# A one-layer streaming encoder step: gain as a column on transposed rows, first weight blocks in halves, key loads split into groups

## Chip, cores, metric

One core of a Trainium2 chip runs the whole kernel. The metric is device time in microseconds, the median of repeated executions; the profile is of one further execution.

## The reference

One layer of a hybrid encoder on 512 prompt rows and 64 sample rows of width 1024 (float32):

```python
h = rmsnorm(x, g_mix)                        # x * rsqrt(mean(x^2)) * g_mix
rq, rk, rv, rg, dq, dk, dv, gr, gd = split(h @ w_in)       # w_in: 1024 x 8192
dq, dk = rmsnorm per head (g_q, g_k)         # 4 heads, 2 maps of 128
o_r = chunkwise retention(rq, rk, rv)
o_d = differential attention(dq, dk, dv)     # sample rows also see 512 cached keys
x = x + (sig(gr) * out_r + sig(gd) * out_d) @ w_out
x = x + hier_moe(rmsnorm(x, g_ffn))          # 16 experts, two for each row
```

Outputs are y, the new keys and values, and the retention states.

## The kernel before

Rows are in five tiles of 128 (`TT` = 5; tile 4, `PT`, holds the 64 sample rows). Products are made in a split float32 form: each operand is stored as a high part (rounded to fp32r) and a low part (the rest), and `product` (L467) issues three matmuls, high by high, low by high, high by low. For tile 4 high and low rows lie side by side in one stationary operand, so two matmuls do (L1792, L1793).

The 8192 columns of `w_in` are taken as 16 chunks of 512 columns. A chunk has two 1 MB blocks, numbered n = 2c and 2c + 1, each with 4 of the 8 contraction steps. SyncE loads blocks into four slots of `raw`; ScalarE rounds a block to `w_hi` (`dense_hi`, L393), VectorE subtracts to `w_lo` (`dense_lo`, L402, written in place), TensorE uses it for five tiles (`dense`, L1771: 24 matmuls for a tile, 16 for tile 4).

Before the first chunk the input is prepared. VectorE multiplies each tile of `x_tok` by the gain `gmix`, spread over all partitions, into one of two `h_tok` buffers (`gained`, L1271). TensorE transposes it in two halves of four 128 x 128 transposes (`source`, L1757; `ident` is the first part of the constant tile `gen`), ScalarE copies each half from PSUM to `s_hi` (`source_hi`), VectorE makes `s_lo` (`source_lo`). The order on each engine is written out by hand: TensorE does tiles 0 and 1, then `dense` of tile 0, the transposes of tiles 2 and 3, `dense` of tile 1, the transposes of tile 4. The row norm (`x_rstd`, from squares that ScalarE sums, `square_x`) is applied later, as a scale when ScalarE evacuates a product (`evacuate_z`, L913), so no product leaves PSUM before it is there. After it VectorE clears three staging regions and casts two constants (L1298 to L1300), and then works on chunk 0: for each of the first tiles a square and a reduce, and the low parts of blocks 2 and 3 behind tiles 1 and 2. Products alternate between PSUM banks 0 and 1.

Chunks 8 to 11 are interleaved with attention: unit g = 5h + t does for head h and tile t the transposed mix of the unit before, `scores`, a share of the transposes of the next head's queries and keys (`head_part`; parts 0 to 6, at t = 1: 0 and 1, t = 2: 2 and 3, t = 3: 4 and 5, t = 4: 6), then `dense` for one tile and the weighted values of the unit before. Parts 0 and 3 read the prompt keys `k_tok`, 1 and 4 the cached keys `kc_tok`, 2 and 5 the prompt queries `q_tok`, 6 the sample rows of both. These tiles exist once, so the loads for head h + 2 (`load_keys`, L632: four DMAs, issued by GpSimd) wait until part 6 of head h + 1 is evacuated, in the unit with t = 4, ahead of that unit's store of its product. TensorE waits before part 0 for all four:

```python
        def head_part(h, k):
            if k == 0:
                pe.wait_ge(kq_in, 64 * (h + 1))
```

After attention come retention, the output products, routing and the 16 experts. At the very end GpSimd waits for the last scattered rows (`all_landed(0)`, L861).

Of the kernel before, what the change touches and what calls it, by code (L numbers as in the profile page):

```python
# [14 lines left out]
P = 128  # L15
D_MODEL = 1024
PROMPT = 512
# [96 lines left out]
def build(nc, a, o):  # L114
# [55 lines left out]
    h_tok = after("h_tok", [P, 2, D_MODEL], f32)  # L170
    gmix = after("gmix", [P, D_MODEL], f32)
# [129 lines left out]
    gmix_in, gen_in, x_scaled = sem("gmix_in"), sem("gen_in"), sem("x_scaled")  # L301
# [9 lines left out]
    kq_in, lam_loaded = sem("kq_in"), sem("lam_loaded")  # L311
# [205 lines left out]

    def source_unit(s, t):
        return 2 * TT * s + 2 * (ORDER.index(t) if s == 4 else t)
# [9 lines left out]
    def _(sp):  # L529
        def dense_load(n):  # L530
            if n == LAST:
                sp.wait_ge(state_stored, 32 * H)
            elif n > LAST:
                sp.wait_ge(src_ready, 3 * TT)
# [79 lines left out]
        with sp.If(passes > 1):  # L614
            with sp.Fori(1, passes) as j:
                expert_pass(j)


    @block.gpsimd
    def _(pool):  # L620
# [10 lines left out]

        def load_keys(h):  # L632
            lo, up = h * DV, (h + 1) * DV
            dma(k_tok[:, 0:PT, :], tiles(z["k"], lo, up, 0, PT)).then_inc(kq_in, 16)
            dma(k_tok[0:SAMPLE, PT, :], z["k"][PROMPT:REAL, lo:up]).then_inc(kq_in, 16)
            dma(kc_tok[:, :, :], a["cache_k"][0, 0, :, h, :].rearrange("(t p) c -> p t c", p=P)).then_inc(kq_in, 16)
            dma(q_tok[:, :, :], tiles(z["q"], lo, up)).then_inc(kq_in, 16)
# [57 lines left out]
        for u in range(TT * PURE, TT * IN_CHUNKS):  # L695
# [3 lines left out]
            if g < UNITS:  # L699
                if t == PT and h + 2 < H:  # L700
                    pool.wait_ge(tr_evacuated, small_n["head", h + 1, HEAD_USES - 1] + 1)
                    load_keys(h + 2)
                if t == 1:
                    if h == 0:
                        for s in range(3):
                            pool.wait_ge(stage_stored[s], stored(PURE - 1, s))
                    else:
                        pool.wait_ge(av_ready, TT * h)
                        load_cached_values(h)
                    if h + 1 < H:  # L710
# [12 lines left out]
                if g == 16:  # L723
                    pool.wait_ge(av_ready, 15)
                    for k in range(TT):
                        pool.wait_ge(ring_stored[k], 32)
                    load_ret_values(0)
            else:
                r = g - UNITS
                h = r // TT  # L730
                if r == 1:
                    pool.wait_ge(av_ready, UNITS)
                    load_state(0)
                    load_ret_values(1)
                if r in (2, 7):
                    pool.wait_ge(kw_ready, h + 1)
                    pool.wait_ge(tr_evacuated, small_n["ret", h, 2] + 1)
                    load_ret_keys(h + 2)
                if t == 0 and h >= 1:
                    pool.wait_ge(state_evacuated, TT * h)  # L740
                    load_state(h)
                    if h + 1 < H:
                        load_ret_values(h + 1)
                    store_states(h - 1)
                if r == 17:
                    pool.wait_ge(kw_ready, H)
# [21 lines left out]
        pool.wait_ge(src_ready, 2 * TT)  # L768
# [4 lines left out]
        pool.wait_ge(src_ready, 3 * TT)  # L773
# [87 lines left out]
        all_landed(0)  # L861
# [3 lines left out]
    def _(act):  # L865
# [9 lines left out]
        def lower_half(bank):  # L875
            nc.scalar.copy(fold[:, :], ps[SAMPLE:P, bank, :]).then_inc(fold_ready, 1)  # L876

# [30 lines left out]
        root()  # L908
        source_hi(0, 4)
# [3 lines left out]
        def evacuate_z(c, t):  # L913
# [15 lines left out]
            if t < PT:  # L929
                nc.scalar.activation(dst[:, t, :], ps[:, u % 2, :], func,  # L930
                                     scale=x_rstd[:, t:t + 1]).then_inc(z_evacuated, 1)
            else:
                if c:
                    act.wait_ge(z_evacuated, TT * c)
                lower_half(u % 2)
# [299 lines left out]
    def _(dve):  # L1235
# [27 lines left out]
        def sum_dense(c):  # L1263
            sum_halves((TT * c + PT) % 2, c).then_inc(folded, 1)
# [6 lines left out]
        def gained(t):  # L1271
            dve.wait_ge(x_in[t], 16)
            if t == PT:
                dve.wait_ge(x_padded, 1)
            if t >= 2:
                dve.wait_ge(src_transposed, 2 * (t - 1))
            v.tensor_tensor(h_tok[:, t % 2, :], x_tok[:, t, :], gmix[:, :], ALU.mult).then_inc(src_ready, 1)
# [17 lines left out]
        source_lo(0, 4)  # L1295
# [221 lines left out]
        def router_weights():  # L1517
            dve.wait_ge(router_in, 80)
            dve.wait_ge(src_ready, 2 * TT)
# [234 lines left out]
    def _(pe):  # L1754
        mm, transpose = nc.tensor.matmul, nc.tensor.transpose

        def source(s, t, src):  # L1757

            for half in range(2):
# [3 lines left out]
                deep = 3 if s == 0 else 2  # L1763
                if u >= deep:
                    pe.wait_ge(slo_ready, u - deep + 1)
# [5 lines left out]
        def dense(s, c, t, ready, within=None):  # L1771
# [4 lines left out]
            pe.wait_ge(slo_ready, 2 * TT * s + 2 * (t + 1))  # L1776
            if u >= 2:
                if u < TT * IN_CHUNKS + 2:
# [3 lines left out]
            bank, rows = ps[:, u % 2, :], slice(t * P, (t + 1) * P)  # L1782
            for k in range(KC):
# [3 lines left out]
                if t == 0 and kk == 0:  # L1787
                    pe.wait_ge(lo_ready, n + 1)
# [7 lines left out]
                if k == 3 and within is not None:  # L1796
                    route(within)
# [19 lines left out]
        def head_part(h, k):  # L1817
            if k == 0:
                pe.wait_ge(kq_in, 64 * (h + 1))
# [65 lines left out]
        pe.wait_ge(gen_in, 16)  # L1885

        def first_source(t):
            pe.wait_ge(src_ready, t + 1)
            source(0, t, h_tok[:, t % 2, :])

        first_source(0)
        first_source(1)
        for c in range(PURE):
            for t in range(TT):
# [3 lines left out]
                dense(0, c, t, z_ready)  # L1898
                if c == 0:
                    for k in ((2, 3), (4,), (), (), ())[t]:  # L1900
                        first_source(k)
# [58 lines left out]
        def attended_source(t):  # L1960
            pe.wait_ge(src_ready, TT + t + 1)
# [19 lines left out]
        def next_source(x, t):  # L1981

            if x == 1:
                pe.wait_ge(src_ready, 2 * TT + t + 1)
# [40 lines left out]
        for n, t in enumerate(ORDER):  # L2025
            dense(3, IN_CHUNKS + 4, t, p_ready, within=n)
# [143 lines left out]
_INS = ["x_prompt", "x_sample", "cache_k", "cache_v", "state_ret", "g_mix", "w_in", "g_q", "g_k", "lambda_q1",  # L2170
# [24 lines left out]
```

## Time and profile before

| what | value |
|---|---|
| median of 3 runs | 1052.09 us (1050.88 to 1052.38) |
| profiled execution | 1057.25 us, of which its span is 1055.4 us |
| TensorE busy | 1012.0 us, 96% of the span |
| VectorE busy | 677.4 us, 64% |
| ScalarE busy | 529.0 us, 50% |
| GpSimd busy | 146.7 us, 14% |
| mean granted TensorE clock | 0.985 of full |

TensorE is busy nearly all the time, so the places to look at are the few where it is not. Times below count from the start of the span. A difference between two kernels' spans is set against the difference of their medians, since the profiled execution is some 5 us longer than the median.

### The profile page before, as it was taken

The numbers are of one execution on the slowest core, as the hardware profiler recorded it, in microseconds if no ns is written. First come the engines' busy times: TensorE is split into PE (matmuls) and PEld (weight loads), VectorE is DVE, ScalarE is ACT, GpSimd is POOL, SyncE is SP. The second block draws the span as 40 slices with busy tenths as digits, with TensorE's granted clock in tenths as the row PEclk, the third lists the DMA queues.
The fourth block names the chain that finished last, engine by engine and source line by source line (L and its number), as shares of the span: only waits on it lengthen the run. The fifth ranks groups of instructions, "written<-read, shape, count | busy, mean of one in ns | idle before, by whom it ended". The sixth has DMA issues, their size and how long they took to land.

```text
span 1055.4 us, 12423 instructions
## 1 busy us (share of the span) xinstructions
PE 1012.0 (96%) x4780; PEld 832.6 (79%) x4780; DVE 677.4 (64%) x990; ACT 529.0 (50%) x726; POOL 146.7 (14%) x181
## 2 busy tenths in 40 slices
PE   4999999999999999999999999998999999999996
PEld 3788888888777888788778888887778888888784
DVE  5677775226555664345246655687699898888882
ACT  4433322446454554333353223364587877868772
POOL 1000011111202121211112000011211211212112
PEclk9999999999999999999999999998899999999998
DMA  9238856262615334424347434227799999999994
GB/s 304 67 143 305 306 216 221 94 247 86 215 41 210 112 143 140 141 110 160 125 160 262 157 125 160 101 102 270 303 425 381 405 384 404 396 392 405 383 368 63
DMA packets 62180, 238.20 MB, mean 226 GB/s; under 512 B 5392, under 2 KB 5568, under 8 KB 49792
## 3 DMA queue, kind: packets, MB, share of 16 engines
q1 hardware_dynamic: 41152, 163.32, 40.5%
q0 software_dynamic: 20960, 73.99, 21.1%
q8 instruction: 40, 0.66, 0.2%
q14 instruction: 28, 0.23, 0.1%
HBM read 199.92 MB, written 48.15 MB: 235 GB/s over the span
## 4 chain that ended last, share of the span: by engine, by line
PE 62%; issue 25%; DMA 5%; POOL 3%; DVE 3%; ACT 1%; SPq 0%; POOLq 0%; ACTq 0%; DVEq 0%
PE ps L469 15%; PE ps L471 15%; PE ps L470 15%; PE ps L1792 3%; PE ps L1793 3%; PE ps L1811 2%; DMA q_tok<-z_q 2%; PE ps L1768 2%; PE ps L1848 1%; POOL x_exp L800 1%; POOL out_y L811 1%; DMA rows_a<-x_slots 1%; DMA x_tok<-in_x_prompt 1%; PE ps L1941 1%; PE ps L1957 1%
## 5 line engine op out<-in xcount | busy, mean ns | idle before, releaser
L469 PE MATMUL ps<-w_hi,s_hi 128*128 128x512 f32 x672 | 268.1, 399 | 1.4 <-ACT stage L930 1.1
L471 PE MATMUL ps<-w_lo,s_hi 128*128 128x512 f32 x672 | 263.4, 392 | 0.0
L470 PE MATMUL ps<-w_hi,s_lo 128*128 128x512 f32 x672 | 263.2, 392 | 0.0
L469 PEld LDWEIGHTS ps<-w_hi,s_hi 128*128 128x128 f32 x672 | 127.4, 190 | 27.5 <-DVE s_hi L1255 1.4
L471 PEld LDWEIGHTS ps<-w_lo,s_hi 128*128 128x128 f32 x672 | 126.9, 189 | 26.9
L470 PEld LDWEIGHTS ps<-w_hi,s_lo 128*128 128x128 f32 x672 | 127.2, 189 | 25.5 <-issue 0.2
L930 ACT ACTIVATE stage<-ps,x_rstd 128x512 f32<-128x512 f32 x64 | 43.9, 688 | 188.3 <-PE ps L471 188.3
L405 DVE TENSOR_TENSOR w_lo<-raw,w_hi 128x2048 fp32r<-128x2048 f32 x42 | 96.2, 2290 | 44.6 <-ACT w_hi L400 44.4
L400 ACT CAST w_hi<-raw 128x2048 fp32r<-128x2048 f32 x42 | 80.0, 1909 | 15.3 <-DMA raw<-in_w_in 10.0
L441 DVE TENSOR_TENSOR lo_x<-raw_x,w_hi 128x2048 fp32r<-128x2048 f32 x32 | 72.1, 2287 | 10.8 <-ACT w_hi L418 10.8
L441 DVE TENSOR_TENSOR lo_x<-raw_x,hi_x 128x2048 fp32r<-128x2048 f32 x32 | 72.2, 2287 | 8.6 <-ACT hi_x L418 8.5
L471 PE MATMUL ps<-lo_x,x_hi 128*128 128x512 f32 x192 | 75.7, 394 | 0.0
L418 ACT CAST w_hi<-raw_x 128x2048 fp32r<-128x2048 f32 x32 | 60.4, 1916 | 16.3 <-DMA raw_x<-in_w_down 12.9
L811 POOL DMA_INDIRECT out_y<-y_exp,s_idx x15 | 35.5, 2363 | 237.7 <-ACT y_exp L1186 237.7
L418 ACT CAST hi_x<-raw_x 128x2048 fp32r<-128x2048 f32 x32 | 60.3, 1916 | 13.2 <-DMA raw_x<-in_w_down 12.4
L1792 PE MATMUL ps<-w_hi,s_hi 128*128 128x512 f32 x168 | 66.6, 396 | 0.0
L1793 PE MATMUL ps<-w_lo,s_hi 128*128 128x512 f32 x168 | 65.5, 390 | 0.0
L469 PE MATMUL ps<-w_hi,x_hi 128*128 128x512 f32 x136 | 54.8, 403 | 1.4 <-issue 1.2
L470 PE MATMUL ps<-w_hi,x_lo 128*128 128x512 f32 x136 | 54.2, 399 | 0.0
L884 ACT CAST s_hi<-ps 128x512 fp32r<-128x512 f32 (+1 forms) x50 | 25.3, 546 | 54.8 <-PE ps L1768 54.5
L469 PE MATMUL ps<-hi_x,x_hi 128*128 128x512 f32 x128 | 51.0, 398 | 1.2 <-DVE x_lo L1690 0.7
L1261 DVE TENSOR_TENSOR fold<-ps,fold 64x512 f32<-64x512 f32 x22 | 15.0, 681 | 52.0 <-ACT fold L876 52.0
(306 smaller groups left out, 1859.2 us busy)
## 6 DMA issues: line engine op xcount, KB each, us to landing
raw<-in_w_in SPq DMA_DIRECT2D x32, 1024.0 KB, 7.3
raw_x<-in_w_up SPq DMA_DIRECT2D x30, 1024.0 KB, 20.4
raw_x<-in_w_down SPq DMA_DIRECT2D x18, 1024.0 KB, 20.8
raw<-in_w_gate SPq DMA_DIRECT2D x16, 1024.0 KB, 19.2
raw_x<-in_w_gate SPq DMA_DIRECT2D x16, 1024.0 KB, 19.8
raw<-in_w_down SPq DMA_DIRECT2D x14, 1024.0 KB, 21.6
x_slots<-in_c_empty SPq DMA_DIRECT2D x4, 2112.0 KB, 16.4
x_exp<-x_slots POOLq DMA_DIRECT2D x16, 528.0 KB, 13.0
```

What stands on the lines that cost most here:

```text
L400: nc.scalar.copy(hi_slots[dense_hi_at(n)], raw_slots[dense_raw(n)]).then_inc(hi_ready, 1)
L405: nc.vector.tensor_tensor(lo_slots[dense_raw(n)], raw_slots[dense_raw(n)], hi_slots[dense_hi_at(n)].bitcast(f32), ALU.subtract).then_inc(l ...
L418: nc.scalar.copy(hi_of(i, q), raw_of(i, q)).then_inc(hi_ready, 1)
L441: nc.vector.tensor_tensor(lo_of(i, q), raw_of(i, q), hi_of(i, q).bitcast(f32), ALU.subtract).then_inc(lo_ready, 1)
L469: nc.tensor.matmul(out, s_h, w_h, start=first, stop=False)
L470: nc.tensor.matmul(out, s_l, w_h, start=False, stop=False)
L471: return nc.tensor.matmul(out, s_h, w_l, start=False, stop=last)
L811: pool.indirect_dma_start(out=y_dram, out_offset=bass.IndirectOffsetOnAxis(ap=s_idx[:, i:i + 1], axis=0), in_=y_exp[i % 2][:, :], in_offse ...
L884: nc.scalar.copy(s_hi[:, 4 * half:4 * half + 4, t * P:t * P + rows], ps[:, source_bank(u), :].rearrange("p (k c) -> p k c", k=4)[:, :, 0:r ...
L930: nc.scalar.activation(dst[:, t, :], ps[:, u % 2, :], func, scale=x_rstd[:, t:t + 1]).then_inc(z_evacuated, 1)
L1792: mm(bank, s_hi[:, k, rows], w_h, start=k == 0, stop=False)
L1793: last = mm(bank, s_hi[:, k, rows], w_l, start=False, stop=k == KC - 1)
```

## The change

In the prologue the gain is no longer applied to rows. TensorE transposes `x_tok` itself, and VectorE multiplies each transposed half in PSUM by the gain as a column (`gmix_col`, 128 partitions x 8) into one of four buffers `h_half`; `s_hi` and `s_lo` are made from there. The identity is loaded alone, ahead of the rest of `gen`. Blocks 0 and 1 are loaded, rounded and subtracted in halves with semaphores of their own. Tile 1 is transposed in the middle of the first tile's product, tiles 2, 3 and 4 behind tiles 0, 1 and 2. Eight transposes of the identity follow those of tile 0. Chunk 0 has a PSUM bank for each tile. Key loads are split: prompt keys in the unit with t = 3, cached keys and prompt queries in that with t = 4 behind part 5, sample rows behind part 6 with a semaphore of their own. At the end SyncE waits for the scattered rows in place of GpSimd. `src_ready` counts five less everywhere, since it is no longer raised in the prologue.

```diff
+    def z_bank(u):
+        return u if u < TT else u % 2
...
+        def first_load(n):
+            for half, landed in enumerate((raw_early[n], raw_full[n])):
+                sp.dma_start(raw[:, n, half * (BLK // 2):(half + 1) * (BLK // 2)].rearrange("p (k c) -> p k c", k=2),
+                             chunk_block(n)[:, 2 * half:2 * half + 2, :]).then_inc(landed, 16)
         load_x(0)
-        sp.dma_start(gmix[:, :], a["g_mix"][0].partition_broadcast(P)).then_inc(gmix_in, 16)
-        dense_load(0)
-        sp.dma_start(gen[:, :], a["c_gen"]).then_inc(gen_in, 16)
+        sp.dma_start(ident, a["c_gen"][:, 0:P]).then_inc(ident_in, 16)
+        sp.dma_start(gmix_col[:, :], a["g_mix_col"]).then_inc(gmix_in, 16)
+        first_load(0)
         load_x(1)
-        dense_load(1)
+        first_load(1)
         load_x(2)
         load_x(3)
         sp.dma_start(x_tok[0:SAMPLE, PT, :], a["x_sample"][0]).then_inc(x_in[PT], 16)
+        sp.dma_start(gen[:, P:], a["c_gen"][:, P:]).then_inc(gen_in, 16)
...
+        sp.wait_ge(y_half_landed, 16)
+        for k in range(2):
+            sp.wait_ge(y_scattered[k], 16 * (NE // 2))
...
+                if t == 3 and h + 2 < H:
+                    pool.wait_ge(tr_evacuated, small_n["head", h + 1, 3] + 1)
+                    load_prompt_keys(h + 2)
                 if t == PT and h + 2 < H:
+                    pool.wait_ge(tr_evacuated, small_n["head", h + 1, 5] + 1)
+                    load_cached_keys(h + 2)
+                    load_prompt_queries(h + 2)
                     pool.wait_ge(tr_evacuated, small_n["head", h + 1, HEAD_USES - 1] + 1)
-                    load_keys(h + 2)
+                    load_sample_keys(h + 2)
...
-        all_landed(0)
...
-        dense_hi(act, 0)
-        source_hi(0, 0)
-        dense_hi(act, 1)
+        first_hi(0, 0)
+        gained_hi(0)
+        gained_hi(1)
+        first_hi(0, 1)
+        gained_hi(2)
+        first_hi(1, 0)
+        gained_hi(3)
+        first_hi(1, 1)
         act.wait_ge(x_padded, 1)
         square_x(0)
-        source_hi(0, 1)
+        gained_hi(4)
+        gained_hi(5)
         square_x(1)
         square_x(2)
+        gained_hi(6)
+        gained_hi(7)
         square_x(3)
-        source_hi(0, 2)
         square_x(4)
-        source_hi(0, 3)
+        gained_hi(8)
+        gained_hi(9)
         root()
-        source_hi(0, 4)
...
+        def gained(u):
+            half = u % 2
+            dve.wait_ge(src_transposed, u + 1)
+            if u >= 4:
+                dve.wait_ge(slo_ready, u - 3)
+            v.tensor_tensor(h_half[:, u % 4, :, :], ps[:, source_bank(u), :].rearrange("p (k c) -> p k c", k=4),
+                            gmix_col[:, 4 * half:4 * half + 4].unsqueeze(2).to_broadcast([P, KC // 2, P]),
+                            ALU.mult).then_inc(x_gained, 1)
...
         dve.wait_ge(gmix_in, 16)
         gained(0)
         gained(1)
-        dense_lo(dve, 0)
-        source_lo(0, 0)
-        dense_lo(dve, 1)
-        source_lo(0, 1)
+        first_lo(0, 0)
+        gained_lo(0)
+        gained_lo(1)
+        first_lo(0, 1)
         gained(2)
         gained(3)
-        source_lo(0, 2)
-        gained(4)
-        source_lo(0, 3)
+        first_lo(1, 0)
+        gained_lo(2)
+        gained_lo(3)
+        first_lo(1, 1)
+        for u in (4, 6, 8):
+            gained(u)
+            gained(u + 1)
+            gained_lo(u)
+            gained_lo(u + 1)
         dve.wait_ge(x_squared, TT)
...
-        source_lo(0, 4)
...
+        pe.wait_ge(ident_in, 16)
         first_source(0)
-        first_source(1)
+        for k in range(8):
+            transpose(ps[:, 4, (k % 4) * P:(k % 4 + 1) * P], ident, ident)
...
+                if c == 0 and t < 3:
+                    dense(0, c, t, z_ready, within=(lambda: first_source(1)) if t == 0 else None)
+                    first_source(t + 2)
```

## Rows read from the trace of the kernel before

**Rows 1.** Waits of TensorE over the run: in total, times, longest

```profile
PE ps L1811 <- DMA q_tok<-z_q: 4.5, 2, 2.5
```

**Rows 2.** POOL, then ScalarE, about unit 3; landing of the q_tok loads

```profile
262.49 0.54 POOL L753 DMA_DIRECT2D z_rv<-stage  x1 [8.31 <-ACT stage L930]
...
271.89 0.89 POOL L637 DMA_DIRECT2D q_tok<-z_q  x1
...
259.31 0.60 ACT L945 COPY qT<-ps 128x512 f32<-128x512 f32 x1
...
DMA to landing us min/median/max: 8.1/10.0/10.9
```

**Rows 3.** TensorE in units 1, 6 and 11: scores, then the next mix; a window's clock

```profile
236.56 1.03 PE L1848 MATMUL ps<-kT,qT 128*128 128x256 f32 x4
...
244.26 0.38 PE L1811 MATMUL ps<-gen,prob 128*128 128x128 f32 x2
...
279.32 1.03 PE L1848 MATMUL ps<-kT,qT 128*128 128x256 f32 x4
...
291.11 0.38 PE L1811 MATMUL ps<-gen,prob 128*128 128x128 f32 x2
...
326.10 1.03 PE L1848 MATMUL ps<-kT,qT 128*128 128x256 f32 x4
...
337.49 0.38 PE L1811 MATMUL ps<-gen,prob 128*128 128x128 f32 x2
...
279.00:284.00 5.00, 2.50 (x13) 0.86 0.91 326
```

**Rows 4.** Issues of the prologue, KB, us to landing; last, landing of gffn_col

```profile
x_tok<-in_x_prompt SPq DMA_DIRECT2D x1, 512.0 KB, 3.6
...
gmix<-in_g_mix SPq DMA_DIRECT2D x1, 512.0 KB, 5.3
...
raw<-in_w_in SPq DMA_DIRECT2D x1, 1024.0 KB, 9.1
...
raw<-in_w_in SPq DMA_DIRECT2D x1, 1024.0 KB, 12.0
...
gffn_col<-in_g_ffn_col POOLq DMA_DIRECT2D x1, 4.0 KB, 10.5
```

**Rows 5.** Timeline of the prologue up to the last transposes

```profile
10.77 1.90 ACT L400 CAST w_hi<-raw 128x2048 fp32r<-128x2048 f32 x1 [8.75 <-DMA raw<-in_w_in]
11.31 1.97 PE L1768 MATMUL ps<-gen,h_tok 128*128 128x128 f32 x8 [11.31 <-DMA gen<-in_c_gen]
...
15.92 1.28 DVE L1255 TENSOR_TENSOR s_lo<-ps,s_hi 128x512 fp32r<-128x512 f32 x2
...
17.43 0.78 PE L469 MATMUL ps<-w_hi,s_hi 128*128 128x512 f32 x1
...
18.43 0.63 PE L471 MATMUL ps<-w_lo,s_hi 128*128 128x512 f32 x1
...
32.09 1.04 PE L1768 MATMUL ps<-gen,h_tok 128*128 128x128 f32 x8
```

**Rows 6.** Timeline from the root's table load to the end of chunk 0

```profile
27.85 1.28 ACT L873 ACT_TABLE_LOAD   x1
...
34.15 0.48 DVE L1298 MEMSET stage<- 64x512 f32 x1 [0.16 <-issue]
34.27 0.47 PE L469 MATMUL ps<-w_hi,s_hi 128*128 128x512 f32 x1 [1.14 <-ACT stage L930]
...
39.39 2.29 DVE L405 TENSOR_TENSOR w_lo<-raw,w_hi 128x2048 fp32r<-128x2048 f32 x1
...
43.04 2.29 DVE L405 TENSOR_TENSOR w_lo<-raw,w_hi 128x2048 fp32r<-128x2048 f32 x1
...
48.63 0.39 PE L1793 MATMUL ps<-w_lo,s_hi 128*128 128x512 f32 x1
```

**Rows 7.** The last compute instruction of the timeline

```profile
1046.26 1.54 POOL L818 DMA_INDIRECT out_y<-y_exp,s_half  x1 [1.44 <-ACT y_exp L1186]
```

More of the change, by code:

```diff
@@ L169, in build @@
     x_tok = at("x_tok", [P, TT, D_MODEL], f32, X + 30720)
-    h_tok = after("h_tok", [P, 2, D_MODEL], f32)
-    gmix = after("gmix", [P, D_MODEL], f32)
+    h_half = after("h_half", [P, 4, KC // 2, P], f32)
+    gmix_col = after("gmix_col", [P, KC], f32)
     sq_x = at("sq_x", [P, D_MODEL], f32, X + 98304)
@@ L300, in build @@
     hi_ready, lo_ready, blocks_used = sem("hi_ready"), sem("lo_ready"), sem("blocks_used")
-    gmix_in, gen_in, x_scaled = sem("gmix_in"), sem("gen_in"), sem("x_scaled")
+    gmix_in, ident_in, gen_in, x_scaled = sem("gmix_in"), sem("ident_in"), sem("gen_in"), sem("x_scaled")
+    raw_early, hi_early, lo_early = [sem("raw_early0"), sem("raw_early1")], sem("hi_early"), sem("lo_early")
+    x_gained = sem("x_gained")
     rot_in, ret_in, router_in = sem("rot_in"), sem("ret_in"), sem("router_in")
@@ L310, in build @@
     ring_stored = [sem(f"ring_stored{t}") for t in range(TT)]
-    kq_in, lam_loaded = sem("kq_in"), sem("lam_loaded")
+    kq_in, kq_rest_in, lam_loaded = sem("kq_in"), sem("kq_rest_in"), sem("lam_loaded")
     v_in, vc_in = [sem("v_in0"), sem("v_in1")], sem("vc_in")
@@ L533, in dense_load @@
             elif n > LAST:
-                sp.wait_ge(src_ready, 3 * TT)
+                sp.wait_ge(src_ready, 2 * TT)
             elif n >= WR:
@@ L630, in _, with load_prompt_keys, load_cached_keys, load_prompt_queries @@
         dma(r_bias[:, NG:NG + NE], a["b_expert"][0].partition_broadcast(P)).then_inc(rot_in, 16)
-        def load_keys(h):
[L633 to L637, printed above, removed]
+        def load_prompt_keys(h):
+            dma(k_tok[:, 0:PT, :], tiles(z["k"], h * DV, (h + 1) * DV, 0, PT)).then_inc(kq_in, 16)
+        def load_cached_keys(h):
+            dma(kc_tok[:, :, :], a["cache_k"][0, 0, :, h, :].rearrange("(t p) c -> p t c", p=P)).then_inc(kq_in, 16)
+        def load_prompt_queries(h):
+            dma(q_tok[:, 0:PT, :], tiles(z["q"], h * DV, (h + 1) * DV, 0, PT)).then_inc(kq_in, 16)
+        def load_sample_keys(h):
+            lo, up = h * DV, (h + 1) * DV
+            dma(k_tok[0:SAMPLE, PT, :], z["k"][PROMPT:REAL, lo:up]).then_inc(kq_rest_in, 16)
+            dma(q_tok[:, PT, :], z["q"][PROMPT:ROWS, lo:up]).then_inc(kq_rest_in, 16)
+        def load_keys(h):
+            load_prompt_keys(h)
+            load_cached_keys(h)
+            load_prompt_queries(h)
+            load_sample_keys(h)
         def load_values(h):
@@ L767, in _ @@
         dma(gffn[:, :], a["g_ffn"][0].partition_broadcast(P)).then_inc(router_in, 16)
-        pool.wait_ge(src_ready, 2 * TT)
+        pool.wait_ge(src_ready, TT)
         dma(count_up[:, :], a["c_count"]).then_inc(router_in, 16)
@@ L772, in _ @@
         dma(w_r[:, :, NG:NG + NE], a["w_expert"][0].rearrange("(k p) c -> p k c", p=P)).then_inc(router_in, 16)
-        pool.wait_ge(src_ready, 3 * TT)
+        pool.wait_ge(src_ready, 2 * TT)
         load_gate("gr", 1, 2)
@@ L876, in lower_half, with first_hi, gained_hi @@
             nc.scalar.copy(fold[:, :], ps[SAMPLE:P, bank, :]).then_inc(fold_ready, 1)
+        def first_hi(n, half):
+            cols = slice(half * (BLK // 2), (half + 1) * (BLK // 2))
+            act.wait_ge(raw_full[n] if half else raw_early[n], 16)
+            nc.scalar.copy(w_hi[:, n, cols], raw[:, n, cols]).then_inc(hi_ready if half else hi_early, 1)
+        def gained_hi(u):
+            t, half = divmod(u, 2)
+            rows = P if t < PT else SAMPLE
+            act.wait_ge(x_gained, u + 1)
+            nc.scalar.copy(s_hi[:, 4 * half:4 * half + 4, t * P:t * P + rows], h_half[:, u % 4, :, 0:rows])\
+                .then_inc(shi_ready, 1)
         def source_hi(s, t):
@@ L929, in evacuate_z @@
             if t < PT:
-                nc.scalar.activation(dst[:, t, :], ps[:, u % 2, :], func,
+                nc.scalar.activation(dst[:, t, :], ps[:, z_bank(u), :], func,
                                      scale=x_rstd[:, t:t + 1]).then_inc(z_evacuated, 1)
@@ L934, in evacuate_z @@
                     act.wait_ge(z_evacuated, TT * c)
-                lower_half(u % 2)
+                lower_half(z_bank(u))
                 act.wait_ge(folded, c + 1)
@@ L1263, in sum_dense @@
         def sum_dense(c):
-            sum_halves((TT * c + PT) % 2, c).then_inc(folded, 1)
+            sum_halves(z_bank(TT * c + PT), c).then_inc(folded, 1)
         own(v.memset(stat[:, :, :, :], 1.0))
@@ L1268, in _, with gained_lo, first_lo @@
         v.memset(x_tok[SAMPLE:P, PT, :], 0.0).then_inc(x_padded, 1)
[L1271 to L1277, printed above, removed]
+        def gained(u):
[6 more added lines that the diff above has]
+                            ALU.mult).then_inc(x_gained, 1)
+        def gained_lo(u):
+            t, half = divmod(u, 2)
+            ks, rows = slice(4 * half, 4 * half + 4), P if t < PT else SAMPLE
+            hi = s_hi[:, ks, t * P:t * P + rows]
+            lo = s_lo[:, ks, t * P:t * P + rows] if t < PT else s_hi[:, ks, t * P + rows:t * P + 2 * rows]
+            dve.wait_ge(x_gained, u + 1)
+            dve.wait_ge(shi_ready, u + 1)
+            v.tensor_tensor(lo, h_half[:, u % 4, :, 0:rows], hi.bitcast(f32), ALU.subtract).then_inc(slo_ready, 1)
+        def first_lo(n, half):
+            cols = slice(half * (BLK // 2), (half + 1) * (BLK // 2))
+            dve.wait_ge(hi_ready if half else hi_early, n + 1)
+            v.tensor_tensor(w_lo[:, n, cols], raw[:, n, cols], w_hi[:, n, cols].bitcast(f32), ALU.subtract)\
+                .then_inc(lo_ready if half else lo_early, 1)
         dve.wait_ge(gmix_in, 16)
@@ L1518, in router_weights @@
             dve.wait_ge(router_in, 80)
-            dve.wait_ge(src_ready, 2 * TT)
+            dve.wait_ge(src_ready, TT)
             own(v.tensor_tensor(w_r[:, :, :], w_r[:, :, :], gffn_col[:, :].unsqueeze(2).to_broadcast([P, KC, NR]),
@@ L1762, in source @@
                     pe.wait_ge(tr_evacuated, len(small))
-                deep = 3 if s == 0 else 2
-                if u >= deep:
-                    pe.wait_ge(slo_ready, u - deep + 1)
+                if s == 0 and u >= 3:
+                    pe.wait_ge(x_gained, u - 2)
+                elif s:
+                    pe.wait_ge(slo_ready, u - 1)
                 for k in range(4):
@@ L1775, in dense @@
             ends = t == (ORDER[-1] if x >= 4 else PT)
-            pe.wait_ge(slo_ready, 2 * TT * s + 2 * (t + 1))
-            if u >= 2:
-                if u < TT * IN_CHUNKS + 2:
+            if u:
+                pe.wait_ge(slo_ready, 2 * TT * s + 2 * (t + 1))
+            if u >= TT:
+                if u < TT + 2:
+                    pe.wait_ge(z_evacuated, u - 3)
+                elif u < TT * IN_CHUNKS + 2:
                     pe.wait_ge(z_evacuated, u - 1)
@@ L1781, in dense @@
                     pe.wait_ge(p_evacuated, u - TT * IN_CHUNKS - 1)
-            bank, rows = ps[:, u % 2, :], slice(t * P, (t + 1) * P)
+            bank, rows = ps[:, z_bank(u), :], slice(t * P, (t + 1) * P)
             for k in range(KC):
@@ L1786, in dense @@
                 w_h, w_l = hi_slots[dense_hi_at(n)][:, cols], lo_slots[dense_raw(n)][:, cols]
-                if t == 0 and kk == 0:
+                if u == 0 and kk == 0:
+                    pe.wait_ge(slo_ready, half + 1)
+                    pe.wait_ge(lo_early, n + 1)
+                if t == 0 and kk == (2 if u == 0 else 0):
                     pe.wait_ge(lo_ready, n + 1)
@@ L1796, in dense @@
                 if k == 3 and within is not None:
-                    route(within)
+                    within()
             if not ends:
@@ L1818, in head_part @@
             if k == 0:
-                pe.wait_ge(kq_in, 64 * (h + 1))
+                pe.wait_ge(kq_in, 48 * (h + 1))
+            if k == HEAD_USES - 1:
+                pe.wait_ge(kq_rest_in, 32 * (h + 1))
             if k < 6:
@@ L1882, in weighted_values @@
             last.then_inc(av_ready, 1)
-        pe.wait_ge(gen_in, 16)
         def first_source(t):
-            pe.wait_ge(src_ready, t + 1)
-            source(0, t, h_tok[:, t % 2, :])
+            pe.wait_ge(x_in[t], 16)
+            if t == PT:
+                pe.wait_ge(x_padded, 1)
+            source(0, t, x_tok[:, t, :])
+        pe.wait_ge(ident_in, 16)
         first_source(0)
-        first_source(1)
+        for k in range(8):
+            transpose(ps[:, 4, (k % 4) * P:(k % 4 + 1) * P], ident, ident)
         for c in range(PURE):
@@ L1897, in _ @@
                         head_part(0, k)
[L1898 to L1901, printed above, removed]
+                if c == 0 and t < 3:
+                    dense(0, c, t, z_ready, within=(lambda: first_source(1)) if t == 0 else None)
+                    first_source(t + 2)
+                else:
+                    dense(0, c, t, z_ready)
         for g in range(UNITS):
@@ L1960, in attended_source @@
         def attended_source(t):
-            pe.wait_ge(src_ready, TT + t + 1)
+            pe.wait_ge(src_ready, t + 1)
             source(1, t, od[:, t, :])
@@ L1983, in next_source @@
             if x == 1:
-                pe.wait_ge(src_ready, 2 * TT + t + 1)
+                pe.wait_ge(src_ready, TT + t + 1)
                 source(2, t, ro[:, t, :])
@@ L2025, in _ @@
         for n, t in enumerate(ORDER):
-            dense(3, IN_CHUNKS + 4, t, p_ready, within=n)
+            dense(3, IN_CHUNKS + 4, t, p_ready, within=lambda: route(n))
             if n == 0:
@@ L2167, in stored @@
     return sum(32 if SECTION[k][0] in ("k", "v") else 16 for k in range(min(c + 1, PURE)) if k % 3 == s)
-_INS = ["x_prompt", "x_sample", "cache_k", "cache_v", "state_ret", "g_mix", "w_in", "g_q", "g_k", "lambda_q1",
+_INS = ["x_prompt", "x_sample", "cache_k", "cache_v", "state_ret", "w_in", "g_q", "g_k", "lambda_q1",
         "lambda_k1", "lambda_q2", "lambda_k2", "g_ret", "w_ret_o", "g_sub", "w_diff_o", "w_out", "g_ffn", "w_group",
@@ L2182 @@
     arrays, ins = {}, {}
-    by_row = {"g_ffn_col": inputs["g_ffn"].reshape(KC, P).T}
+    by_row = {"g_mix_col": inputs["g_mix"].reshape(KC, P).T, "g_ffn_col": inputs["g_ffn"].reshape(KC, P).T}
     for name, arr in [(n, inputs[n]) for n in _INS] + list(by_row.items()) + list(shape_constants().items()):
```

## Prediction

> **What bounds the kernel now.** I read the shares of the page first: TensorE works 96% of the span, so no other engine's saving counts unless it closes a gap of TensorE's. Then its waits, then the timeline at each. Three kinds matter here. It does nothing for the first 11.3 us and reaches the first product at 17.43 [rows 5]. It waits 4.5 us in two places for the load of the queries [rows 1]. And its matmuls are slow for a while behind a gap. Everything else is back to back, so a gap closed at 280 us should be kept to the end.
>
> **The key loads.** Units 1, 6 and 11 do the same work (tile 1 of heads 0, 1, 2, each with parts 0 and 1 of the next head). From scores to the next mix unit 1 takes 244.26 - 236.56 = 7.70 us, unit 6 takes 291.11 - 279.32 = 11.79 and unit 11 takes 337.49 - 326.10 = 11.39 [rows 3]. Units 6 and 11 contain the two waits [rows 1]. The excess is 4.09 + 3.69 = 7.8 us: 4.5 of waiting, and 3.3 of matmuls and transposes at the lower clock behind it (granted clock 0.86 in the mean over 279 to 284, that is, partly at 1.2 in place of 2.4 GHz [rows 3]). What does the change do to it? The query load was issued at 271.89, last of four, behind part 6 of unit 4. It is now the second of two behind part 5, whose evacuation ended at 259.9; GpSimd gets there when its store of unit 3 is issued, 262.49 + 0.54, so the queries go out at 263.03 + 0.8 = 263.8, 8.1 us sooner; prompt keys a whole unit before that [rows 2]. With the slowest landing, 10.9 us, they are there at 274.7; TensorE wants them at 280.4. A margin of 5.7 us: both waits go, and with them the slow stretches. I take the whole 7.8. The lower bound is the waits without the clock, 4.5. The new waits of GpSimd are for evacuations that are over when it comes to them, so the stores queued behind (z_rv) go out no later; behind part 6 two DMAs are issued where there were four, so that store goes about 2 us sooner. Heads 0 and 1 cost one DMA more each, 0.5 us of GpSimd, long before use. The wait for the sample rows stands at part 6, three units behind part 0. What is late next in units 6 and 11? The same unit in head 0 shows no wait, and the weight blocks were loading together with the keys (DMA share 0.91 in the row [rows 3]), which now pass earlier; I find nothing.
>
> **The prologue, start.** Landings: x of tile 0 at 0.74 + 3.6 = 4.3, gain at 1.20 + 5.3 = 6.5, block 0 at 10.8, block 1 at 15.2 [rows 4, 5]. In the queue the gain (512 KB) and the constants (218 KB) stood ahead of what is needed; now 64 KB and 4 KB do. So the first half of block 0 ends about where the gain ended, 512 KB behind x: 6.5, I take 6.9 for the two small loads; its second half 2.1 later (half of the 4.3 from gain to block 0), 9.0. For the column nothing like it is in the trace but gffn_col, of the same 128 rows of 32 bytes, 10.5 us on GpSimd's queue [rows 4]. Bounds: issued at 1.65, it lands between 5.3 (with the 3.6 of x) and 12.2; I take 6, since little stands ahead of it.
>
> The ladder: transposes from about 4.8, 8 at low clock take 1.97 [rows 5], halves ready at 5.9 and 6.8. The multiply from PSUM over 128x512 should cost what the subtraction from PSUM does, 0.65 [rows 5]: 6.65 and 7.5. ScalarE rounds a half block (half of 1.90, about 1.0) to 7.9, VectorE subtracts it (half of 2.29, 1.15) to 9.05, the low half tile to 9.7. **TensorE starts its product at 9.75, 7.7 us sooner than at 17.43.** Its first six matmuls at 0.43 apart (17.99 to 18.43 and on, slow [rows 5]) last to 12.3, six more at full rate to 13.7; VectorE has the second half block ready by 11.6. Full rate is 0.228: 64 matmuls of tiles 2 to 4 from 34.27 to 48.86 [rows 6].
>
> **The prologue, the return.** Now tile 1 is transposed (halves ready 14.3, 14.75), VectorE multiplies both (15.6), ScalarE rounds the first (15.55), and only then the first half of block 1 (16.6): low part 17.75. TensorE has stood since about 14.8, 3 us. Six matmuls, slow again, to 20.4; the second half of block 1 is ready at 20.2 (VectorE has two low half tiles in between, 0.65 each); the last six end at 22.4. Call this E. Neither x of tile 1 nor block 1 is late in it: block 1 landed at 15.2 even before [rows 4].
>
> Behind E: transposes (1.0 for 8 [rows 5]), tile 1 (24 x 0.228 = 5.46), transposes, tile 2, then tile 4's transposes at E + 12.9, now one tile later than before. Call it T. VectorE multiplies its halves (T + 2.0), ScalarE rounds them (T + 2.45), loads the root's table (1.28 [rows 6]), and the root gives x_rstd at T + 4.2. VectorE clears from T + 4.35. From there the low part of block 2 ended 39.39 + 2.29 - 34.15 = 7.5 later and that of block 3 11.2 later [rows 6]: T + 11.9 and T + 15.5. TensorE has only 1.0 + 5.46 + 3.64 = 10.1 us of chunk 0 left behind T. **So chunk 1 waits: 1.8 us for block 2, 1.0 for block 3.** Before, chunk 1 began at 48.86 with both ready since 45.3 [rows 6]. Now it goes as if begun at T + 15.5 - 2.73 = E + 25.7 = 48.1. Net gain of the whole prologue: 0.8 us, of the 7.7 at the start. The separate banks keep TensorE from the wait of 1.14 at 34.27 [rows 6] (counted, since I run chunk 0 without it). Bounds: if the first matmuls run at full clock, E is 20.4 and the gain 2.8; if the column lands at 12.2, product 0 begins at 14.1, E is near 27 and the prologue loses 3.8.
>
> On the eight transposes of the identity: before, TensorE ran transposes from 11.31 on, with gaps, and the matmuls at 17.43 and 18.43 were still slow [rows 5]. So I count no help from them. The page "TensorE: Matmul & The Clock Gate" of the Trainium skill, in its section "PE-mode transpose", says that transposes do not count as busy for the clock gate the way matmuls do. By that rule the eight are of no use and the forecast stands; if they count, it is the case of 2.8. The trace agrees with the page so far.
>
> **The end.** The last instruction begins at 1046.26, the span ends 9.1 us later [rows 7]; its landing must be waited for by someone. Which engine waits I price at nought; bounds 0 to 1 us of gain, since only the engines' closing steps could overlap with it.
>
> **Sum.** 7.8 + 0.8 = 8.6 us. Profiled execution: 1057.25 - 8.6 = 1048.6, span 1046.8. That execution stands 5.2 us over the median; I take the difference over: 1052.1 - 8.6 = **1043.5**.
>
> **Rivals.**
> (a) The start is kept: the clock is up at the first product. For it: sixteen transposes without a gap, where there were eight. Against: the slow matmuls at 17.43 behind transposes [rows 5]. 7.8 + 2.8: 1041.5. Chance 0.17.
> (b) The column is late, as gffn_col. 7.8 - 3.8 = 4.0: 1048.1. Against it: loads in the prologue land when the bytes ahead of them have passed, and only 0.6 MB are ahead of the column; the 10.5 us of gffn_col for 4 KB must be mostly other loads' time. Chance 0.09.
> (c) The queries' wait goes but another, of a block's split or a value load, takes half of it: 3.9 + 0.8: 1047.4. Chance 0.07.
> (d) The other side: the ladder of TensorE, VectorE, ScalarE, VectorE on each half tile repeats for tiles 2 to 4 and pushes the root, and with it blocks 2 and 3, back. It decides when E or T comes 8.6 us later than I have them (E at 31). That needs each of some eight handovers at double its price, against rows of 0.65 and 1.0 us: 1053 or more. Chance 0.03 slower, 0.03 for no change.
> The forecast, 0.61, its own range 1042.3 to 1045.
>
> A measurement of this kernel tells about 0.2%, 2.1 us, from no change. All but (d) is faster by more: 0.94, 0.03, 0.03. The range: from (a) with the gain at the end, 1040.7, to most of the way to (c), 1046.5.
>
> **What would show it.** Right: no wait of L1811 for q_tok; units 6 and 11 near 7.7 us; first product near 9.8; a gap of 3 us in the middle of tile 0; a gap at the start of chunk 1 with VectorE's low part as its releaser. Wrong: gmix_col as a releaser; a wait near 280; chunk 1 starting without a gap.

## Result and the profile after

| | before | changed |
|---|---|---|
| median, 12 runs each | 1052.03 us (1049.84 to 1057.29) | 1047.94 us (1046.07 to 1050.50) |
| ratio, 95% interval | 1 | 0.995 (0.9935 to 0.9965) |
| profiled execution | 1057.25 us, span 1055.4 | 1049.38 us, span 1047.5 |

The change is worth 4.1 us by the medians and 0.5%, 5.3 us (3.7 to 6.8), by the ratio; 8.6 were forecast. The two profiled executions differ by 7.9. That is nearly the forecast, and it misleads: the profiled execution of before took 1057.25 us, and of the kernel's 12 others only one took longer (1057.29). It stood 5.2 us over its median; that of the changed kernel stands 1.4 us over.

TensorE's waits of the changed kernel (in total, times, longest), where [rows 1] stood before:

```profile
PE ps L1843 <- DMA gen<-in_c_gen: 4.7, 1, 4.7
PE ps L471 <- DVE w_lo L1345: 3.3, 1, 3.3
...
PE ps L471 <- DVE w_lo L407: 1.8, 1, 1.8
...
PE ps L471 <- DVE s_lo L1340: 1.6, 1, 1.6
```

No wait for q_tok is left. Three new ones, all in the prologue, name VectorE. TensorE's timeline shows them in place, first the products of tile 0 (start, duration, in brackets the idle time before and what ended it), then the transposes of tiles 2 and 4 and the first product of chunk 1:

```profile
4.72 1.97 PE L1843 MATMUL ps<-gen,x_tok 128*128 128x128 f32 x8 [4.72 <-DMA gen<-in_c_gen]
...
10.03 0.80 PE L471 MATMUL ps<-w_hi,s_hi 128*128 128x512 f32 x1 [1.64 <-DVE s_lo L1340]
...
14.89 0.63 PE L473 MATMUL ps<-w_lo,s_hi 128*128 128x512 f32 x1
15.32 1.37 PE L1843 MATMUL ps<-gen,x_tok 128*128 128x128 f32 x8
...
19.99 0.76 PE L471 MATMUL ps<-w_hi,s_hi 128*128 128x512 f32 x1 [3.29 <-DVE w_lo L1345]
...
24.13 1.04 PE L1843 MATMUL ps<-gen,x_tok 128*128 128x128 f32 x8
...
36.81 1.04 PE L1843 MATMUL ps<-gen,x_tok 128*128 128x128 f32 x8
...
48.77 0.47 PE L471 MATMUL ps<-w_hi,s_hi 128*128 128x512 f32 x1 [1.84 <-DVE w_lo L407]
```

The product starts at 10.0 where [rows 5] had 17.43, and it is given back step by step: still at 0.63 a matmul (the low clock) at 14.89, 3.29 us of waiting in the middle of tile 0, 1.84 at chunk 1. VectorE behind it, the clears and the low parts of blocks 2 and 3, beside [rows 6]:

```profile
41.09 0.48 DVE L1372 MEMSET stage<- 64x512 f32 x1 [0.16 <-issue]
...
46.33 2.29 DVE L407 TENSOR_TENSOR w_lo<-raw,w_hi 128x2048 fp32r<-128x2048 f32 x1
...
49.98 2.29 DVE L407 TENSOR_TENSOR w_lo<-raw,w_hi 128x2048 fp32r<-128x2048 f32 x1
```

Units 6 and 11 beside [rows 3], and the issue of the queries beside [rows 2]:

```profile
280.98 1.03 PE L1931 MATMUL ps<-kT,qT 128*128 128x256 f32 x4
...
288.57 0.38 PE L1892 MATMUL ps<-gen,prob 128*128 128x128 f32 x2
...
323.59 1.03 PE L1931 MATMUL ps<-kT,qT 128*128 128x256 f32 x4
...
331.16 0.38 PE L1892 MATMUL ps<-gen,prob 128*128 128x128 f32 x2
```
```profile
264.66 0.76 POOL L651 DMA_DIRECT2D kc_tok<-in_cache_k  x1
265.41 0.76 POOL L654 DMA_DIRECT2D q_tok<-z_q  x1
```

Both units take 7.6 us. The queries go out 15.6 us ahead of unit 6's scores, where before it was 7.4.

### The profile page after: what moved, and what is told of

It is laid out like the page before. It is cut to its first block, busy times and chain, and to the rows that moved or that the text cites. A ratio compares the mean times of both kernels' runs of the same rounds, so it can differ in the third digit from the quotient of the medians.

```text
span 1047.5 us, 12470 instructions
## 1 busy us (share of the span) xinstructions
PE 1014.2 (97%) x4788; PEld 835.0 (80%) x4788; DVE 678.3 (65%) x997; ACT 529.4 (51%) x728; POOL 147.6 (14%) x185
## 4 chain that ended last, share of the span: by engine, by line
PE 63%; issue 25%; DVE 3%; POOL 3%; ACT 1%; POOLq 0%; ACTq 0%; DVEq 0%
PE ps L471 15%; PE ps L473 15%; PE ps L472 15%; PE ps L1873 3%; PE ps L1874 3%; PE ps L1892 2%; PE ps L1931 2%; PE ps L1843 2%; POOL x_exp L834 1%; POOL out_y L845 1%; PE ps L2027 1%; PE ps L2043 1%; PE ps L2034 1%; PE ps L1935 1%; PE ps L2013 1%
## 5 line engine op out<-in xcount | busy, mean ns | idle before, releaser
L472 PEld LDWEIGHTS ps<-w_hi,s_lo 128*128 128x128 f32 x672 | 127.7, 190 | 25.7 <-issue 0.2
L407 DVE TENSOR_TENSOR w_lo<-raw,w_hi 128x2048 fp32r<-128x2048 f32 x40 | 91.6, 2290 | 42.0 <-ACT w_hi L402 41.7
L402 ACT CAST w_hi<-raw 128x2048 fp32r<-128x2048 f32 x40 | 76.2, 1909 | 5.9 <-DMA raw<-in_w_out 3.3
L443 DVE TENSOR_TENSOR lo_x<-raw_x,w_hi 128x2048 fp32r<-128x2048 f32 x32 | 72.1, 2287 | 10.6 <-ACT w_hi L420 10.6
L845 POOL DMA_INDIRECT out_y<-y_exp,s_idx x15 | 35.0, 2333 | 237.6 <-ACT y_exp L1238 237.6
L472 PE MATMUL ps<-hi_x,x_lo 128*128 128x512 f32 x120 | 47.2, 394 | 0.0
## 6 DMA issues: line engine op xcount, KB each, us to landing
raw_x<-in_w_gate SPq DMA_DIRECT2D x16, 1024.0 KB, 19.4
```

Source lines behind the costliest of these rows:

```text
L402: nc.scalar.copy(hi_slots[dense_hi_at(n)], raw_slots[dense_raw(n)]).then_inc(hi_ready, 1)
L407: nc.vector.tensor_tensor(lo_slots[dense_raw(n)], raw_slots[dense_raw(n)], hi_slots[dense_hi_at(n)].bitcast(f32), ALU.subtract).then_inc(l ...
L443: nc.vector.tensor_tensor(lo_of(i, q), raw_of(i, q), hi_of(i, q).bitcast(f32), ALU.subtract).then_inc(lo_ready, 1)
L472: nc.tensor.matmul(out, s_l, w_h, start=False, stop=False)
L845: pool.indirect_dma_start(out=y_dram, out_offset=bass.IndirectOffsetOnAxis(ap=s_idx[:, i:i + 1], axis=0), in_=y_exp[i % 2][:, :], in_offse ...
```

## Experiments

All ratios are to the kernel before, run on the same chip, with 95% intervals; "traces" are one profiled execution for each kernel. `before_copy`, the same program as before, came out at 1.0012 (1.0000 to 1.0024), so a difference of 0.1% in a ratio says nothing.

**The parts alone.** `keys_only` is the kernel before with the key loads of the change; `prologue_only` is the changed kernel with the key loads and the final wait of before; `end_only` is the kernel before with the final wait on SyncE; `before_copy` is unchanged.

```diff
 keys_only (to before)
+                if t == 3 and h + 2 < H:
+                    pool.wait_ge(tr_evacuated, small_n["head", h + 1, 3] + 1)
+                    load_prompt_keys(h + 2)
...
 prologue_only (to the changed kernel)
-                    load_sample_keys(h + 2)
+                    load_keys(h + 2)
...
 end_only (to before)
-        all_landed(0)
+        sp.wait_ge(y_half_landed, 16)
```

> The kernel before with only the key loads split into groups. Theory A (the whole difference between the profiled spans, 7.9 us, is the key loads; the prologue gives nothing): 7 to 8 us faster than before in the median, waits on q_tok gone, units 6 and 11 at 7.7 us from scores to the next mix. Theory B (the profiled execution of before was a long one; in most executions the waits for the queries are shorter, or no slow stretch stands behind them): the waits gone, but only 4 to 6 us faster in the median.

> The changed kernel with the key loads and the final wait as before, so that only the prologue is changed. Theory A: nothing in the median (within 1 us of before). Theory B (the prologue loses what its trace shows, 1.6 us at the start of unit 1, by two further slow stretches of the clock): 1.5 to 2 us slower than before. My prediction had 0.8 us faster.

> The kernel before with only the final wait moved from GpSimd to SyncE. By my prediction nothing (0 to 1 us faster). The profiled spans of before and after differ by 2 us behind the last expert's gate; if that is this wait, the median falls by 1 to 2 us; if it is chance of one execution, by nothing.

> The kernel before, unchanged, to see how much one execution differs from another. If the two waits for the queries with their slow stretches are typical, units 6 and 11 take 11.4 to 11.8 us again and the span is near 1050 to 1055 us. Theory B expects them shorter, 9 to 10.5 us, in this trace. Ratio to before 1.000 within 0.2%.

| kernel | median us | ratio (interval) |
|---|---|---|
| keys_only | 1048.73 | 0.9951 (0.9938 to 0.9964) |
| prologue_only | 1054.40 | 1.0007 (0.9995 to 1.0019) |
| end_only | 1053.20 | 0.9998 (0.9986 to 1.0010) |
| before_copy | 1054.51 | 1.0012 (1.0000 to 1.0024) |

The key loads alone are worth 0.49%, 5.2 us (3.8 to 6.5). The prologue alone, for which the table has +0.7 us (0.5 faster to 2.0 slower), gives no gain that can be seen and may cost. The final wait can't be told from nothing. The product of the three ratios is 0.9956, the changed kernel's own is 0.995. Theory B holds for the keys. It shows in the trace of before_copy, first its waits, then units 6 and 11, then TensorE's clock (the third column behind the window) in the stretches behind the waits:

```profile
PE ps L1811 <- DMA q_tok<-z_q: 3.1, 2, 1.8
```
```profile
279.98 1.03 PE L1848 MATMUL ps<-kT,qT 128*128 128x256 f32 x4
...
289.00 0.38 PE L1811 MATMUL ps<-gen,prob 128*128 128x128 f32 x2
...
324.03 1.03 PE L1848 MATMUL ps<-kT,qT 128*128 128x256 f32 x4
...
333.66 0.38 PE L1811 MATMUL ps<-gen,prob 128*128 128x128 f32 x2
```
```profile
284.00:288.00 4.00, 4.00 (x20) 1.00 0.42 161
...
330.00:335.00 5.00, 5.00 (x25) 1.00 0.03 10
```

The same program, and the two units take 9.02 and 9.63: over unit 1's 7.70 that is 3.3 us, not 7.8. The waits are 1.2 and 1.8 us in place of 2.5 and 2.0, and the clock did not fall behind them. In the profiled execution of before it fell behind both, as the same windows of its trace show:

```profile
284.00:288.00 4.00, 4.00 (x16) 0.74 0.27 110
...
330.00:335.00 5.00, 5.00 (x18) 0.66 0.37 139
```

Two more kernels have the old key loads. In the trace of prologue_only one of the two waits drew a slow stretch and the other didn't: units of 11.41 and 9.57 us, 5.6 us over unit 1's. In that of end_only neither did: waits of 1.68 and 1.71 us, units of 9.48 and 9.51, 3.6 us. So what the key loads cost before varies from one execution to the next, by the four traces from 3.3 to 7.8 us; their mean, 5.1, fits the timed 5.2, and the trace that the forecast was read from is the highest of the four.

**Where the keys' gain comes from.** `keys_late` is the kernel before with the loads in the new pieces and with the separate wait, but all issued behind part 6:

```diff
 keys_late (to before; the unit with t = 4 still calls load_keys behind part 6)
         def load_keys(h):
...
+            load_prompt_keys(h)
+            load_cached_keys(h)
+            load_prompt_queries(h)
+            load_sample_keys(h)
...
-                pe.wait_ge(kq_in, 64 * (h + 1))
+                pe.wait_ge(kq_in, 48 * (h + 1))
+            if k == HEAD_USES - 1:
+                pe.wait_ge(kq_rest_in, 32 * (h + 1))
```

> The kernel before with the key loads in the new pieces (queries ahead of the sample rows, a semaphore of its own for these) but all issued where they were, behind part 6. The queries are then issued some 0.5 us sooner than before, not 8 us. If the place of the issue is what counts (my prediction), the waits shrink by about 0.5 us each and the median falls by 1 to 2 us; if the order of the pieces is enough, both waits go and the median falls by 5 us as with the whole change.

Measured: 1051.66 us, 0.9995 (0.9979 to 1.0010). Its waits for q_tok:

```profile
PE ps L1824 <- DMA q_tok<-z_q: 2.1, 2, 1.7
```

Order and pieces alone leave both waits, of 1.7 and 0.4 us in this trace, and the interval of its ratio lies wholly above that of keys_only (0.9938 to 0.9964). The gain needs the earlier issue. Whether the new order gives the 1 to 2 us that were expected of it can't be told: the interval goes from 2.2 us faster to 1.1 slower.

**The two waits that the new prologue makes.** In `blocks_first` ScalarE rounds both halves of block 1 before tile 1's halves, and VectorE subtracts them before it multiplies tile 1. In `clears_early` VectorE's three clears and two casts stand ahead of tile 2's multiplies. `both` has both.

```diff
 blocks_first (ScalarE)
         first_hi(0, 1)
+        first_hi(1, 0)
+        first_hi(1, 1)
         gained_hi(2)
-        first_hi(1, 0)
         gained_hi(3)
-        first_hi(1, 1)
 blocks_first (VectorE)
         first_lo(0, 1)
+        first_lo(1, 0)
+        first_lo(1, 1)
         gained(2)
         gained(3)
-        first_lo(1, 0)
         gained_lo(2)
         gained_lo(3)
-        first_lo(1, 1)
 clears_early (VectorE)
+        dve.wait_ge(gen_in, 16)
+        for s in range(3):
+            own(v.memset(stage[s][SAMPLE:P, PT, :], 0.0))
+        own(v.tensor_copy(tri16[:, :], tri))
+        own(v.tensor_copy(ones16[:, :], ones))
         for u in (4, 6, 8):
...
-        dve.wait_ge(gen_in, 16)
-        for s in range(3):
-            own(v.memset(stage[s][SAMPLE:P, PT, :], 0.0))
-        own(v.tensor_copy(tri16[:, :], tri))
-        own(v.tensor_copy(ones16[:, :], ones))
```

> The changed kernel, with block 1 rounded and subtracted ahead of tile 1's multiplies on ScalarE and VectorE. Theory L (the ladder: block 1's split stood behind tile 1's multiply, which waits for transposes in the middle of the first product): the wait of 3.3 us and the one of 1 to 2 us behind it in tile 0 go, and the slow stretch that follows; the first product ends near 20 in place of 24.1, unit 1 begins 3 to 5 us sooner than 238.5, median 3 to 5 us below the changed kernel's. Theory R (the root, behind tile 4's transposes, sets the start of chunk 1, but moves with them): the same gain, waits at chunk 1 as long as before. If the start of chunk 1 is set by something that doesn't move, less than 1 us.

> The changed kernel, with VectorE's three clears and two casts (2.4 us) moved from behind the root to ahead of tile 2's multiplies, where it is idle. Theory R: the waits at the start of chunk 1 for the low parts of blocks 2 and 3 shrink by 2.4 us of 2.8, and no slow stretch follows: 2.4 to 4 us below the changed kernel. Rival (ScalarE's evacuations and roundings set it as well): under 1.5 us.

> Both of the two: if they are independent, 6 to 8 us below the changed kernel, 1040 to 1042 us where before is 1052; ratio to before 0.989 to 0.991.

| kernel | median us | ratio (interval) |
|---|---|---|
| blocks_first | 1041.23 | 0.9894 (0.9877 to 0.9912) |
| clears_early | 1043.64 | 0.9906 (0.9891 to 0.9922) |
| both | 1040.76 | 0.9882 (0.9865 to 0.9900) |

Against the changed kernel's 0.995 these are 5.9, 4.6 and 7.2 us, each with an uncertainty of some 2.3 us from the two intervals; 3 to 5, 2.4 to 4 and 6 to 8 were expected. TensorE's waits in the first 60 us, of blocks_first and then of both:

```profile
PE ps L471 <- DVE w_lo L407: 2.4, 2, 1.8
PE ps L471 <- DVE s_lo L1340: 1.9, 1, 1.9
PE ps L471 <- DVE w_lo L1345: 0.2, 1, 0.2
```
```profile
PE ps L471 <- DVE s_lo L1340: 1.5, 1, 1.5
PE ps L471 <- DVE w_lo L407: 0.5, 1, 0.5
PE ps L471 <- ACT stage L982: 0.2, 1, 0.2
```

Block 1 first takes the wait in tile 0 from 3.3 to 0.2 and leaves those at chunk 1 (2.4 us; the second trace of the changed kernel, below, has the same 2.4); with the clears early as well, those go to 0.5. That both mechanisms are at work is shown by these waits.

The sizes are less clear. The product of unit 0 is evacuated at 238.3 us in both traces of the changed kernel (the 238.5 of the expectations), at 236.5 in clears_early, 231.3 in blocks_first and 229.8 in both. So the clears gave 1.8 us alone and 1.5 on top of blocks_first, close to the waits that they took away (2.4 to 0.5, with 0.2 for an evacuation that comes in their place). The timed difference is larger, 4.6, but within its uncertainty; what the rest of it is stays open.

Blocks first gave 7.0 at unit 0. Nearly all of it, 6.7 us, is there when tile 0 is done (at 17.45 in place of 24.13), and only part of that is the new order's doing. 3.1 us are the waiting. 1.0 is the slow stretch that stood behind the wait, from 19.4 us on, and came in neither blocks_first nor both. The remaining 2.6 lie ahead of the wait, in the first twelve matmuls and the transposes behind them: there the clock was granted in full at 8.4 us in this execution and at 16.0 in the first trace of the changed kernel. TensorE's program is the same up to there in both, so this part is chance. In the trace of both, where the full clock came at 13.5, tile 0 ends at 18.07. `both` is the fastest version that I have.

**The identity's transposes.**

```diff
 no_identity (to the changed kernel)
-        for k in range(8):
-            transpose(ps[:, 4, (k % 4) * P:(k % 4 + 1) * P], ident, ident)
```

> The changed kernel without the eight transposes of the identity. If transposes don't raise the clock, nothing changes (within 1 us), and the first product is slow for as long as with them; if they do, its first high clock comes 2 us or more later than at 13.6 and 16.2 in the two traces with them, and the time is 1 to 1.5 us more.

> The changed kernel, unchanged, for a second trace of it. Ratio to before 0.995 within 0.2%. The waits of 3.3, 1.8 and 1.0 us in the prologue come again; whether the slow stretches behind them (from 19.6 and from 50.4) come again shows how much of the span is chance of the clock: each of 3.4 us costs 1.7.

Measured: no_identity 1047.91 us, 0.9944 (0.9930 to 0.9957); after_copy 1047.04 us, 0.9946 (0.9927 to 0.9964). The time doesn't tell them apart, so the eight transposes bought nothing that can be measured. But the clock did something for which I had counted no help. TensorE's timeline of after_copy, where its first product begins:

```profile
10.58 0.50 PE L471 MATMUL ps<-w_hi,s_hi 128*128 128x512 f32 x1 [2.35 <-DVE s_lo L1340]
10.92 0.40 PE L472 MATMUL ps<-w_hi,s_lo 128*128 128x512 f32 x1
11.15 0.39 PE L473 MATMUL ps<-w_lo,s_hi 128*128 128x512 f32 x1
...
12.13 0.63 PE L473 MATMUL ps<-w_lo,s_hi 128*128 128x512 f32 x1
```

and of blocks_first:

```profile
6.29 1.91 PE L1977 MATMUL ps<-gen 128*128 128x128 f32 x8
10.09 0.50 PE L471 MATMUL ps<-w_hi,s_hi 128*128 128x512 f32 x1 [1.89 <-DVE s_lo L1340]
10.43 0.40 PE L472 MATMUL ps<-w_hi,s_lo 128*128 128x512 f32 x1
10.66 0.40 PE L473 MATMUL ps<-w_lo,s_hi 128*128 128x512 f32 x1
```

A matmul of 0.39 to 0.40 us is one at 2.4 GHz, one of 0.63 at 1.2 (the granted clock of after_copy is 0.50 from 12 to 14 us). In these two traces the first product ran at the high clock from its first matmul, with only transposes ahead of it; the clock record in the traces has the full grant at 8.1 and 8.4 us. In the other four traces with the eight transposes it came at 13.3 to 16.7, behind the first matmuls, and in the one without them at 14.0. In after_copy the clock fell again at 11.5, three matmuls on, so little was gained: its first twelve matmuls took 4.4 us, against 5.3 in the first trace. In blocks_first it stayed, and they took 3.2. TensorE's program is the same up to there, so this too is chance.

after_copy repeats the wait of 3.3 us in tile 0 and those at chunk 1 (2.4 in all), and unit 0 ends its product at the same 238.3; its slow stretches lay elsewhere, longer in tile 0 and none at 50 us.

## Why the prediction was wrong

The forecast, faster, was right; the size was too large (8.6, where 4.1 or 5.3 was measured) and the median lies above the range.

- **The key loads, forecast 7.8, worth 5.2 (keys_only).** The mechanism was right in each step: the issue moved by 8 us against the scores, both waits went, units 6 and 11 are at 7.6. The step that failed is "I take the whole 7.8": the waits and the slow stretches of one execution were taken for those of the median. The four traces with the old loads have 7.8, 5.6, 3.6 and 3.3, and timing has 5.2. The prediction noted that this execution stood 5.2 us over the median, and took the difference over unchanged; but 3.6 us of it were this very term (7.8 against the 4.2 of the other three traces in the mean), and they went with the change. Its own lower bound, "the waits without the clock, 4.5", was nearer.
- **The start of the prologue, forecast 9.75, measured 10.03.** Right. The first half of block 0 landed at 2.13 + 4.9 = 7.0 (6.9 forecast), and the column at 1.66 + 3.2 = 4.9, sooner than the 6 and even than the bound of 5.3, so rival (b) fell.
- **"Six more at full rate".** All twelve matmuls of the first half were slow: the last began at 14.89, the forecast had it done at 13.7. They took 5.3 us where 3.95 were forecast, 1.3 of the 1.7 us by which E came late (24.1, 22.4 forecast); the rest are differences of 0.3 to 0.5 either way, as the wait in the middle, forecast at 3 us and measured 3.29. In three other traces of the new prologue (prologue_only, no_identity, both) the clock did come up at the seventh or eighth matmul, and E was 23.8, 24.4 and, without the wait, 18.1.
- **Behind E.** The transposes of tile 4 came at E + 12.7 (12.9 forecast), VectorE's clears at T + 4.3 (4.35), the low parts of blocks 2 and 3 ended at T + 11.8 and T + 15.5 (11.9 and 15.5), the wait for block 2 was 1.84 (1.8). With E at 24.1, the forecast's own E + 25.7 is 49.8, later than 48.86: no gain of 0.8, but a loss of 0.9. What it left out is the slow stretch behind this wait in the first trace (matmuls of 0.63 us that began from 50.3 to 52.9), which the second trace did not have.
- **The prologue in all, forecast 0.8 faster, measured 0.7 slower with an interval from 0.5 faster to 2.0 slower.** The product of unit 0 is evacuated at 236.7 to 237.6 in five traces with the old prologue, at 237.2, 237.8, 238.3 and 238.3 in four with the new one: 0.7 us later in the mean, as timed. The 7.7 us of the start are given back in full.
- **The end, forecast nought.** end_only doesn't tell it from nought. In the traces, though, the stretch from the last scatter's start to the end of the span is 9.0 to 9.6 us in five that wait on GpSimd and 7.9 to 8.7 in seven that wait on SyncE: about 1 us, which the timing of end_only neither shows nor rules out (1.5 faster to 1.1 slower).

So 5.2 - 0.7 is 4.5, between the 4.1 and the 5.3 that were measured. (The lower end of the range was added up a little wrong: rival (a) with the gain at the end is 1040.5, not 1040.7.) Rivals (c) and (d) fell too: no other wait came up in units 6 and 11, and the root was not pushed further than forecast. Rival (a) had its clock in two traces of six. Of the changed kernel's own two traces one had it, lost it after three matmuls, and reached unit 0 at the same time as the other; what 2.8 us of gain would have needed, a clock that stays, came in blocks_first alone.

## What to carry to other kernels

Before a gap's price is read off a profile, compare the profiled execution with the median: here it stood 5 us above, and most of the excess (3.6 us, against the other traces with the same loads) sat in the very waits that the change removes. Ask of each gap what it costs with and without the slow clock behind it, and forecast between the two.

When work is cut into pieces to start sooner, write down the order in which each in-order engine meets the pieces: here a weight block that had long landed stood behind a multiply that waited for a transpose in the middle of the product that needed the block. Putting the work that waits for nobody first gave about 6 us (by the ratios, 0.9894 against 0.995, give or take 2.3), as much as the whole change; 3.1 us of waiting and the slow clock behind it are what the trace puts down to the order.

## What the runs showed of the hardware

- Transposes alone can raise TensorE's clock from 1.2 to 2.4 GHz: it was granted in full at 8.1 and 8.4 us in two executions in which nothing but 16 transposes, from 4.5 us on, had run. The Trainium skill ("TensorE: Matmul & The Clock Gate", section "PE-mode transpose") says that the full clock doesn't engage for transposes, since they don't count as busy the way matmuls do. The measurement decides; in four other executions of the same prologue the clock rose only later, behind matmuls.
- The clock behind the same gap differs between executions. Behind the wait of 3.29 us in tile 0 (or within it) it fell in all five traces that have it. Behind the wait of 1.83 to 1.84 us for block 2 it fell in one of five. Behind the waits for the queries it fell after those of 2.50, 2.02 and 1.98 us, and not after those of 1.83, 1.77, 1.71, 1.68 and 1.24.
- Such gaps may be part of what spreads a kernel's time, which no run here separates: before ran from 1049.8 to 1057.3 us in its 12 runs, the changed kernel from 1046.1 to 1050.5. Other parts vary too: from unit 11's mix to the end of the span the twelve traces take 715 to 720 us.
- A load of 128 rows of 32 bytes landed in 3.2 us in the prologue. Its like [rows 4] took 10.5 to 10.6, on GpSimd's queue and issued in the middle of the run among loads of up to 1280 KB; that those loads are the reason is likely, and no run shows it.
